# Attention loop of a hybrid decoder layer: gate products of the merge, two at a time, only ahead of the second head's transposes

## The chip, the cores and the metric

The kernel is one program on one core of a Trainium2 chip. It computes one layer of a hybrid decoder for a prompt of 1024 tokens and 8 single-token samples. The metric is the device time of one execution in microseconds (us). The engines are TensorE (PE in the profile; its weight loads are PEld), VectorE (DVE), ScalarE (ACT), GpSimd (POOL) and SyncE (SP), whose queue issues the DMAs.

## The reference, cut to what matters

Two parts of the layer meet in the stage that is changed: the sparse attention of the prompt, and the sigmoid gate of the merge, whose product with the input does not depend on the attention.

```python
h = rms_norm(x, g_pre_mix) * (1.0 + sc1) + sh1
parts = project(h, w_in, b_in)             # 'ga' and 'gb' are 1024 of its columns each
y_a, y_b, state = mix_fn(parts)            # y_b: the attention, 8 heads of 64 on 2 key groups
merged = jax.nn.sigmoid(parts['ga']) * (y_a @ w_proj_a) + jax.nn.sigmoid(parts['gb']) * (y_b @ w_proj_b)

# in the attention, for blocks of 128 queries, each head sums three softmaxes:
p_c = masked_softmax(q . kc)               # 32 compressed keys
p_s = masked_softmax(q . ks)               # all earlier blocks of keys (the sequence has 16 blocks, top 16 are taken)
p_w = masked_softmax(q . k_win)            # a window of 512 keys
out = g0 * (p_c @ vc) + g1 * (p_s @ vs) + g2 * (p_w @ v_win)
```

## The kernel before

The attention of the prompt is a list of 132 items (`items`, L290), four times 33. A group of 33 belongs to a pair of heads j = 0 to 3. Its first item is the compressed branch of both heads; then come 16 steps k = 0 to 15, each with two items, e = 0 for the first head of the pair and e = 1 for the second. Step k treats the query block i = k // 2: an even k is the window branch, an odd k the selected branch. The number of 128-key blocks (`span_of`, L295) grows with i: 1 at k = 0, 5 in most of the window steps, 8 at k = 15. All is fp32.

Each item n goes through five engines' stations, always in the order of n on every engine:

- `att_S` (L2362): the scores, on TensorE, issued two items ahead;
- `att_max` (L1699): the causal mask and the maximum, on VectorE;
- `att_exp` (L1172): the exponential with its sum, on ScalarE;
- `att_rec` (L1733) and L1015: the reciprocal of the sum on VectorE, then the scaling by it and by the branch's gate on GpSimd;
- `att_T` (L2385): 128x128 transposes of the scaled probabilities on TensorE (L2398; L2395 in the compressed branch), which wait for the scaling;
- `take_T` (L591): the transposed blocks are copied out of PSUM, groups in bank 0 by VectorE and groups in bank 1 by ScalarE (L608, L603). From step k = 8 on an item has two groups, and the first, of four blocks, is in bank 0. Below that an item has one group, and the two items of a step use the two banks in turn, the first head bank 0;
- `att_PV` (L2401): the product with the values for both heads of a step (L2415, L2420), issued once the second head's item has been transposed.

The order on VectorE is written out: for item n it takes the group of bank 0 of item n, then the reciprocal of item n + 1, then the maximum of item n + 2. On ScalarE it is the group of bank 1 of item n, then the exponential of item n + 2, then the tanh of a gate chain if one ended in item n (L1213).

TensorE has further work in this loop that does not depend on it: 18 gate chains (6 slices of 128 output columns by 3 groups of 344 tokens) of 8 products each, 144 products in all (`gate_product`, L2424). A chain accumulates in PSUM bank 7. Its first product waits until the tanh of the chain before has read that bank (`s_filla`). `gates_at`, a table made at L314 to L326, gives to each item two lists of products: those issued ahead of `att_T(n)`, and those issued ahead of `att_S(n + 2)`. The numbers of slots come from `gate_slots` (L309), and `rest` keeps a new chain from starting too soon after the last one ended. SyncE loads the weight slices of the chains into two places by turns, each when three chains have released its place.

In this text a *product* is one matmul of 344 columns; the profile records each fp32 matmul as two instructions, so that a product is "x2" there. T0 is the transposes of a first head's item, T1 those of a second head's.

Of the kernel before, what the change touches and what calls it, by code (L numbers as in the profile page):

```python
# [129 lines left out]
def build(nc, t, outs):  # L130
# [3 lines left out]
    with ExitStack() as ctx:  # L134
# [102 lines left out]
        def take(rows, *shape):  # L237
# [52 lines left out]
        items = [(j, None, None) if k is None else (j, k, e)  # L290
                 for j in range(NH // 2) for k, e in [(None, None)] + [(k, e) for k in range(2 * NT) for e in range(2)]]
        NI = len(items)
# [16 lines left out]
        def gate_slots(n):  # L309
            if items[n][1] is None:  # L310
                return (3, 3) if n == 0 else (3, 0)
            return (1, 3) if n + 2 < NI and items[n + 2][1] is None else (1, 0)

        gates_at, queue, rest = {}, [(c, c // 3, c % 3, k) for c in range(3 * MF) for k in range(KD)], 0  # L314
        for n_ in range(NI):
            gates_at[n_] = ([], [])
            for x, slots_ in enumerate(gate_slots(n_)):
                if slots_ == 1 and queue and queue[0][3] in (0, 6):
                    slots_ = 2

                while slots_ and queue and (queue[0][3] or n_ >= rest):
                    gates_at[n_][x].append(queue.pop(0))
                    slots_ -= 1
                    if gates_at[n_][x][-1][3] == KD - 1:
                        rest = n_ + 2
# [2407 lines left out]
```

How the kernel before makes its waits and increments, by code:

```python
        def freed(eng, rnd, step):  # L558
            g, k = divmod(step, KN[rnd])
            if k < KN[rnd] - 1:
                eng.wait_ge(s_rused, (0, 3 * (KN[0] - 1))[rnd] + g * (KN[rnd] - 1) + k + 1)
            else:
                eng.wait_ge(s_yps, 9 * rnd + 3 * (g + 1))
# [18 lines left out]
        def take_q(eng, copy, j, bank):  # L583
            eng.wait_ge(s_pt[bank], fills_Q[j][bank][1] + 1)
            for e in range(2):
                for half in range(2):
                    ins = copy(qT_[e][half * HD:(half + 1) * HD, bank * 512:(bank + 1) * 512], ps[e * HD:(e + 1) * HD, 4 + bank, :])
            ins.then_inc(s_ev[bank], 1)
# [1 line left out]
        def take_T(eng, copy, t, bank):  # L591
            j, k, e = items[t]
            for b, blocks, turn in fills_T[t][0]:
                if b != bank:
                    continue
                eng.wait_ge(s_pt[b], turn + 1)
                if k is None:
                    if j:
                        eng.wait_ge(s_pv, pv_before(j - 1, 2 * NT - 2) + 1)
                    else:
                        eng.wait_ge(s_kvrows, 32)
                    copy(pcT[b], ps[0:2 * NCMP, 4 + b, :]).then_inc(s_ev[b], 1)
                else:
                    u = unit_at(t)
                    if u >= 3:
                        eng.wait_ge(s_pv, (u - 3) // 2 + 1)
                    copy(ptbuf[u % 3][:, blocks[0]:blocks[-1] + 1, :],
                         ps[:, 4 + b, 0:len(blocks) * P].rearrange("p (o c) -> p o c", c=P)).then_inc(s_ev[b], 1)
```

## Time and profile before

| | |
|---|---|
| time, median of 3 runs | 2107.27 us (2101.02 to 2110.47) |
| the profiled execution | 2108.73 us, its span 2107.0 us |
| TensorE busy | 2020.4 us, 96% of the span |
| VectorE, ScalarE, GpSimd busy | 811.1, 516.6, 389.5 us |
| the chain of work that ended last | TensorE 87%, VectorE 4%, DMA 3%, ScalarE 2%, GpSimd 2% |
| the attention loop | from 466 to 846 us of the span |

The table is read with two things in mind. First, TensorE is close to saturated over the whole program, so that what counts is the idle time on it. Secondly, the share is an average over stages; the attention loop is one of those where TensorE is often released by another engine. In the views of the trace a row of the timeline is a run of like instructions on one engine: its start, its length up to the modelled end of the last, the engine, the line, what it writes and reads, the count, and in brackets the idle time ahead of it with what ended it. Since matmuls overlap, the length of a row is more than what it takes on the engine; the distance between two starts is the better measure.

### The profile page before, as it was taken

The page shows a single profiled execution, that of the slowest core. Times are in us where ns is not written, and L with a number is a line of the kernel's source. Part 1 is how long each engine was busy: PE and PEld are TensorE (multiplying, and loading weights), DVE is VectorE, ACT ScalarE, POOL GpSimd, SP SyncE. Part 2 cuts the span into 40 slices and gives each one's busy share as a digit, 9 for nine tenths or more (in the row PEclk, how much of TensorE's full clock was granted, in tenths as well). Part 3 has the DMA queues.
Part 4 walks back from the last instruction along what each step waited for, and adds up shares of the span by engine and source line. Part 5 has one row for each costly group of instructions (what it writes and reads, how often), then busy time and mean ns, then how long its engine had stood idle before and what let it go on. Part 6 is the DMA issues. An engine that isn't in the chain of part 4 may idle for free.

```text
span 2107.0 us, 28710 instructions
## 1 busy us (share of the span) xinstructions
PE 2020.4 (96%) x11391; PEld 1599.5 (76%) x11391; DVE 811.1 (38%) x1522; ACT 516.6 (25%) x938; POOL 389.5 (18%) x447
## 2 busy tenths in 40 slices
PE   6999999989999998999999998899999999999998
PEld 3588877775665565666676675899999999888876
DVE  2444333475665657521202165411111111234355
ACT  2322210134444444111200145311111111123232
POOL 0000111222232323231000046000000000155552
PEclk8999999999999999999999999999999999999999
DMA  9342001032000000564324354112112112235453
GB/s 361 114 173 101 21 23 40 1 89 80 11 11 11 8 5 11 169 169 115 97 72 130 102 178 150 61 41 60 41 40 61 40 41 61 81 122 167 150 190 111
DMA packets 172941, 184.90 MB, mean 88 GB/s; under 512 B 9893, under 2 KB 143117, under 8 KB 172366
## 3 DMA queue, kind: packets, MB, share of 16 engines
q1 hardware_dynamic: 172814, 183.12, 27.7%
q8 instruction: 91, 1.49, 0.3%
q14 instruction: 36, 0.29, 0.0%
HBM read 170.74 MB, written 16.53 MB: 89 GB/s over the span
## 4 chain that ended last, share of the span: by engine, by line
PE 87%; DVE 4%; DMA 3%; ACT 2%; POOL 2%; issue 1%; SPq 1%; POOLq 0%; ACTq 0%; DVEq 0%
PE ps L2659 23%; PE ps L2560 11%; PE ps L2163 9%; PE ps L2184 5%; PE ps L2602 5%; PE ps L2603 5%; PE ps L2604 5%; PE ps L2430 4%; PE ps L2420 3%; PE ps L2381 3%; PE ps L2398 3%; DMA arena<-in_w_ada 1%; POOL arena L1015 1%; PE ps L2123 1%; DVE arena L608 1%
## 5 line engine op out<-in xcount | busy, mean ns | idle before, releaser
L2659 PE MATMUL ps<-h_hi,wup_hi 128*128 128x344 f32 x1056 | 339.3, 321 | 9.7 <-issue 4.9
L2659 PE MATMUL ps<-h_lo,wup_hi 128*128 128x344 f32 x1056 | 339.8, 322 | 0.0
L2659 PE MATMUL ps<-h_hi,wup_lo 128*128 128x344 f32 x1056 | 339.4, 321 | 0.0
L1046 POOL CAST ra_hi<-arena 128x384 fp32r<-128x384 f32 (+1 forms) x90 | 51.6, 573 | 851.2 <-PE ps L2659 465.7
L2659 PEld LDWEIGHTS ps<-h_hi,wup_hi 128*128 128x128 f32 x1056 | 200.0, 189 | 10.6 <-issue 9.5
L2659 PEld LDWEIGHTS ps<-h_lo,wup_hi 128*128 128x128 f32 x1056 | 199.8, 189 | 0.0
L2602 PE MATMUL ps<-rw_hi,ra_hi 128*128 128x512 f32 x480 | 191.1, 398 | 8.8 <-DVE rw_lo L1885 5.7
L2659 PEld LDWEIGHTS ps<-h_hi,wup_lo 128*128 128x128 f32 x1056 | 199.5, 189 | 0.0
L2163 PE MATMUL ps<-arena,hT 128*128 128x261 f32 (+2 forms) x768 | 194.6, 407 | 3.4 <-ACT hT L1112 2.5
L2603 PE MATMUL ps<-rw_hi,ra_lo 128*128 128x512 f32 x480 | 189.1, 394 | 0.0
L2604 PE MATMUL ps<-rw_lo,ra_hi 128*128 128x512 f32 x480 | 188.3, 392 | 0.0
L2163 PEld LDWEIGHTS ps<-arena,hT 128*128 128x128 f32 x768 | 143.7, 191 | 43.2 <-issue 8.4
L1015 POOL TENSOR_SCALAR arena<-arena 128x640 f32<-128x640 f32 (+7 forms) x128 | 99.9, 781 | 280.4 <-DVE arena L1739 280.4
L1885 DVE TENSOR_TENSOR rw_lo<-hT,rw_hi 128x1024 fp32r<-128x1024 f32 x65 | 91.4, 1410 | 144.6 <-ACT rw_hi L1256 144.6
L2560 PE MATMUL ps<-hT,arena 128*128 128x344 f32 x448 | 134.5, 455 | 0.0
L1189 ACT ACTIVATE arena<-ps,arena 128x640 f32<-128x640 f32 (+7 forms) x128 | 89.6, 700 | 171.1 <-DVE arena L1719 167.7
L1052 POOL TENSOR_TENSOR ra_lo<-arena,ra_hi 128x384 fp32r<-128x384 f32 (+1 forms) x90 | 124.3, 1381 | 4.8
L2560 PEld LDWEIGHTS ps<-hT,arena 128*128 128x128 f32 x448 | 83.9, 190 | 43.6 <-issue 2.1
L2602 PEld LDWEIGHTS ps<-rw_hi,ra_hi 128*128 128x128 f32 x480 | 90.5, 189 | 33.5 <-issue 8.0
L2430 PE MATMUL ps<-hT,xn 128*128 128x344 f32 x288 | 112.0, 497 | 1.3 <-ACT arena L1213 1.2
L2560 PE MATMUL ps<-arena 128*128 128x344 f32 x352 | 112.1, 474 | 0.7 <-ACT arena L1264 0.5
L1256 ACT ACTIVATE rw_hi<-hT 128x1024 fp32r<-128x1024 f32 x65 | 68.7, 1059 | 176.8 <-DMA hT<-in_w_down 176.8
(420 smaller groups left out, 2868.6 us busy)
## 6 DMA issues: line engine op xcount, KB each, us to landing
hT<-in_w_down SPq DMA_DIRECT2D x65, 512.0 KB, 3.3
arena<-in_w_ada SPq DMA_DIRECT2D x12, 2048.0 KB, 8.2
arena<-in_w_up SPq DMA_DIRECT2D x44, 512.0 KB, 4.6
arena<-in_w_out SPq DMA_DIRECT2D x24, 512.0 KB, 3.9
arena<-in_w_in SPq DMA_DIRECT2D x19, 512.0 KB, 4.4
arena<-in_cache_cmp_kv SPq DMA_DIRECT2D x64, 128.0 KB, 2.1
arena<-in_cache_slc_kv SPq DMA_DIRECT2D x128, 64.0 KB, 1.9
arena<-in_w_in SPq DMA_DIRECT2D x4, 1544.0 KB, 13.5
```

The source lines that it names most:

```text
L1015: nc.gpsimd.tensor_scalar(pbuf[u % 3][:, 0:nb * P], pbuf[u % 3][:, 0:nb * P], rec[:, u % 4:u % 4 + 1], gts[:, i, col:col + 1], ALU.mult, A ...
L1052: nc.gpsimd.tensor_tensor(lo[:, 0:n], src[:, k, cols], hi[:, 0:n], ALU.subtract).then_inc(s_ra, 1)
L1189: nc.scalar.activation(pbuf[u % 3][:, 0:n], sp_[:, 512 - n // 2:512 + n // 2], ACT.Exp, bias=nmx[:, u % 4:u % 4 + 1], accum_out=rsum[:, u ...
L1885: nc.vector.tensor_tensor(rw_lo[rnd][at][:, :], rw_from(rnd, step), rw_hi[rnd][at][:, :], ALU.subtract).then_inc(s_rlo, 1)
L2163: ins = nc.tensor.matmul(ps[:, bank, 0:width], hT[:, k, n * P:(n + 1) * P], w[:, k, 0:width], start=(k == 0), stop=(k == KD - 1))
L2184: ins = nc.tensor.matmul(ps[:, mix_bank(j, n), 0:PA], h[:, k, :], w[:, k, :], start=(k == 0 and x == 0), stop=(k == KD - 1 and x == 2))
L2430: ins = nc.tensor.matmul(ps[:, 7, 0:TG], wfill[m % 2][:, k, :], hT[:, k, q * TG:(q + 1) * TG], start=(k == 0), stop=(k == KD - 1))
L2560: ins = nc.tensor.matmul(ps[:, bank, 0:TG], w[:, k, :], src[:, k, q * TG:(q + 1) * TG], start=(k == 0), stop=(k == kn - 1))
L2602: nc.tensor.matmul(out, ra_hi[rnd][a][:, rows], rw_hi[rnd][w][:, cols], start=first, stop=False)
L2603: nc.tensor.matmul(out, ra_lo[rnd][a][:, rows], rw_hi[rnd][w][:, cols], start=False, stop=False)
L2604: ins = nc.tensor.matmul(out, ra_hi[rnd][a][:, rows], rw_lo[rnd][w][:, cols], start=False, stop=last)
L2659: ins = nc.tensor.matmul(ps[:, bank, 0:TG], w[:, k0 + k, :], h[:, k, toks], start=(k == 0 and j == 0), stop=(k == KD - 1 and j == 2))
```

## The change

`gate_slots` gave one slot to every item, and now gives two slots to items with e = 1 and none to items with e = 0. The rule that stretched a slot at the beginning and the end of a chain stretched 1 to 2 at products 0 and 6, and now stretches 2 to 3 at products 0 and 5, so that a chain is issued as 3 + 2 + 3. `rest` keeps its value, but a chain may now start one item sooner after it. The three slots of a compressed item and the three ahead of the scores that cross into the next pair stay.

```diff
         def gate_slots(n):
             if items[n][1] is None:
                 return (3, 3) if n == 0 else (3, 0)
-            return (1, 3) if n + 2 < NI and items[n + 2][1] is None else (1, 0)
+
+            two = 2 * items[n][2]
+            return (two, 3) if n + 2 < NI and items[n + 2][1] is None else (two, 0)
...
-                if slots_ == 1 and queue and queue[0][3] in (0, 6):
-                    slots_ = 2
-
-                while slots_ and queue and (queue[0][3] or n_ >= rest):
+                if slots_ == 2 and queue and queue[0][3] in (0, 5):
+                    slots_ = 3
+
+                while slots_ and queue and (queue[0][3] or n_ >= rest - 1):
```

From this table the 144 products fall out as follows. Before, they stand in 100 runs of one to three, 128 products in the first three pairs and 16 in the fourth, up to its step k = 6. Now they stand in 54 runs of two or three, and all of them are in the first three pairs. The run ahead of the transposes of the second and third pair's compressed item is 2 and 0 products long before, and 3 and 3 now.

TensorE in the second pair, steps k = 11 and 12, from a T0 to the PV behind the next T0. L2398 is the transposes, L2381 the scores, L2415 and L2420 PV, L2430 products. Before:

```order
L2398 MATMUL ps<-const,arena 128x128 x6
L2381 MATMUL ps<-arena 128x320 x2
L2415 MATMUL ps<-arena 64x128 x2
L2420 MATMUL ps<-arena 64x128 x10
L2430 MATMUL ps<-hT,xn 128x344 x2
L2398 MATMUL ps<-const,arena 128x128 x6
L2381 MATMUL ps<-arena 128x320 x2
L2430 MATMUL ps<-hT,xn 128x344
L2398 MATMUL ps<-const,arena 128x128 x5
L2381 MATMUL ps<-arena 128x448 x2
L2420 MATMUL ps<-arena 64x128 x12
```

And now (all lines are two further on):

```order
L2400 MATMUL ps<-const,arena 128x128 x6
L2383 MATMUL ps<-arena 128x320 x2
L2417 MATMUL ps<-arena 64x128 x2
L2422 MATMUL ps<-arena 64x128 x10
L2432 MATMUL ps<-hT,xn 128x344 x2
L2400 MATMUL ps<-const,arena 128x128 x6
L2383 MATMUL ps<-arena 128x320 x2
L2400 MATMUL ps<-const,arena 128x128 x5
L2383 MATMUL ps<-arena 128x448 x2
L2422 MATMUL ps<-arena 64x128 x12
```

The product between the scores behind T1 and the next T0 is gone. (The order has each product once, the trace twice.)

TensorE where the second pair ends and the third begins: the last T0, the transposes of the queries (L2359), products, the compressed scores (L2372), PV, the last T1, and the compressed branch's transposes (L2395). Before:

```order
L2398 MATMUL ps<-const,arena 128x128 x8
L2359 MATMUL ps<-const,arena 128x128 x8
L2430 MATMUL ps<-hT,xn 128x344 x3
L2372 MATMUL ps<-arena 128x32 x16
L2415 MATMUL ps<-arena 64x128 x2
L2420 MATMUL ps<-arena 64x128 x10
L2430 MATMUL ps<-hT,xn 128x344 x2
L2398 MATMUL ps<-const,arena 128x128 x8
L2381 MATMUL ps<-arena 128x64 x2
L2395 MATMUL ps<-const,arena 64x128 x8
```

And now:

```order
L2400 MATMUL ps<-const,arena 128x128 x8
L2361 MATMUL ps<-const,arena 128x128 x8
L2432 MATMUL ps<-hT,xn 128x344 x3
L2374 MATMUL ps<-arena 128x32 x16
L2417 MATMUL ps<-arena 64x128 x2
L2422 MATMUL ps<-arena 64x128 x10
L2432 MATMUL ps<-hT,xn 128x344 x3
L2400 MATMUL ps<-const,arena 128x128 x8
L2383 MATMUL ps<-arena 128x64 x2
L2432 MATMUL ps<-hT,xn 128x344 x3
L2397 MATMUL ps<-const,arena 64x128 x8
```

Three products now stand ahead of the compressed branch's transposes; and the three behind PV begin a new chain, where the two before ended one.

## Rows read from the trace of the kernel before

**Rows 1.** The page's first part: busy time, share of the span, instructions.

```profile
PE 2020.4 (96%) x11391; PEld 1599.5 (76%) x11391; DVE 811.1 (38%) x1522; ACT 516.6 (25%) x938; POOL 389.5 (18%) x447
```

**Rows 2.** Busy time by stretch: engines, granted clock, DMA share, GB/s.

```profile
760.00:780.00 20.00, 17.93 (x128) 11.78 (x128) 11.01 (x37) 7.37 (x25) 3.95 (x8) 0.91 0.01 1
...
800.00:846.00 46.00, 37.06 (x341) 24.24 (x343) 33.16 (x75) 19.46 (x50) 15.07 (x16) 1.00 0.00 1
466.00:846.00 380.00, 352.66 (x2639) 224.09 (x2640) 235.25 (x567) 157.05 (x421) 99.92 (x128) 0.98 0.08 23
```

**Rows 3.** Who waited for whom, 465 to 846 us: total, times, longest.

```profile
PE ps L2398 <- POOL arena L1015: 14.6, 26, 1.0
```

**Rows 4.** The chain that ended last, fourth pair, step k = 9.

```profile
809.05 0.60 PE ps L2398 x4
...
809.68 0.69 DVE arena L608
...
810.54 0.88 POOL arena L1015
```

**Rows 5.** Timeline of TensorE, second pair, k = 11 and 12: start, length, count, idle.

```profile
626.01 0.85 PE L2430 MATMUL ps<-hT,xn 128*128 128x344 f32 x2
626.69 0.82 PE L2398 MATMUL ps<-const,arena 128*128 128x128 f32 x6
...
628.18 0.85 PE L2430 MATMUL ps<-hT,xn 128*128 128x344 f32 x2
629.12 0.76 PE L2398 MATMUL ps<-const,arena 128*128 128x128 f32 x5
...
634.50 0.84 PE L2430 MATMUL ps<-hT,xn 128*128 128x344 f32 x2
635.55 0.98 PE L2398 MATMUL ps<-const,arena 128*128 128x128 f32 x7 [0.20 <-POOL arena L1015]
```

**Rows 6.** The same, two T0 without a product ahead (k = 11, k = 14).

```profile
527.62 0.87 PE L2398 MATMUL ps<-const,arena 128*128 128x128 f32 x6 [0.98 <-POOL arena L1015]
...
642.50 0.76 PE L2398 MATMUL ps<-const,arena 128*128 128x128 f32 x5 [0.76 <-POOL arena L1015]
```

**Rows 7.** The same, at k = 6 and 7: T1 behind two products, then T0.

```profile
597.02 1.42 PE L2430 MATMUL ps<-hT,xn 128*128 128x344 f32 x4
598.28 0.60 PE L2398 MATMUL ps<-const,arena 128*128 128x128 f32 x4
598.81 0.70 PE L2381 MATMUL ps<-arena 64*128 64x256 f32 x4
599.44 0.66 PE L2398 MATMUL ps<-const,arena 128*128 128x128 f32 x4
```

**Rows 8.** Timeline where the third pair begins.

```profile
659.08 1.42 PE L2430 MATMUL ps<-hT,xn 128*128 128x344 f32 x4
659.77 0.60 ACT L1180 ACTIVATE arena<-ps 128x512 f32<-128x512 f32 x1 [4.35 <-DVE ps L1709]
660.34 1.04 PE L2398 MATMUL ps<-const,arena 128*128 128x128 f32 x8
...
663.80 1.92 PE L2395 MATMUL ps<-const,arena 128*64 128x128 f32 x8 [2.06 <-DVE arena L1731]
```

**Rows 9.** The tanh of the gate chains, 600 to 700 us: shortest, median, longest in ns.

```profile
L1213 ACT ACTIVATE arena<-ps,arena x6: 537/538/539, 601.3 to 695.8; 128x344 f32<-128x344 f32 x6
```

**Rows 10.** Timeline at the second pair's k = 1: scores, then the scaling of that item.

```profile
572.25 0.44 PE L2381 MATMUL ps<-arena 64*128 64x64 f32 x4
...
574.15 0.45 POOL L1015 TENSOR_SCALAR arena<-arena 128x128 f32<-128x128 f32 x1 [0.88 <-DVE arena L1739]
```

**Rows 11.** Timeline of TensorE, the fourth pair's head: first T0, then k = 6 and 7.

```profile
768.63 0.27 PE L2398 MATMUL ps<-const,arena 128*128 128x128 f32 x1
...
792.08 0.70 PE L2381 MATMUL ps<-arena 64*128 64x256 f32 x4
...
795.80 0.66 PE L2398 MATMUL ps<-const,arena 128*128 128x128 f32 x4 [0.65 <-POOL arena L1015]
```

## The prediction, made before the changed kernel ran

> **What bounds the kernel now.** I read the page first: TensorE is busy for 96% of the span [rows 1], so any work is dear there, and any idle time. Then the busy times by stretch: in the attention loop, 466 to 846 us, TensorE is busy for 352.66 of 380 us [rows 2]; the idle 27 us are what the order of the gate products can lose or win. The waits say what ends this idle time: above all GpSimd's scaling, ahead of the transposes [rows 3]. The chain that ended last shows how that comes about in the fourth pair, where no products are left. The first four blocks of T1 are followed by VectorE's copy (0.69 us), the reciprocal, GpSimd's scaling (0.88 us) and then T0 [rows 4]. VectorE must copy T1's group before it may take the reciprocal that T0 needs. From T1's start to the end of the scaling this takes 810.54 + 0.88 - 809.05 = 2.37 us, and all that TensorE has to put in between are the rest of T1 and the scores of one item. From T0 to T1 it is the other way round: there PV stands in between, over a us long, and T1 finds its data ready. So from step k = 9 on T0 is the place that waits, and T1 isn't. The change takes the products away from the place that waits and gives them to the one that doesn't.
>
> **What a product costs.** A single product ahead of T1, where nothing is waited for, takes 626.69 - 626.01 = 0.68 us [rows 5]. Two in a row take 598.28 - 597.02 = 1.26 us [rows 7]. So a further product of a run costs 0.58 us, and a run costs 0.10 us on top, for the interruption.
>
> **What the wait of T0 costs.** Without a product ahead the idle time is 0.98 us, and 0.76 us at k = 14, where fewer blocks are scaled [rows 6]. A T that doesn't wait starts before the modelled end of the scores, 599.44 against 598.81 + 0.70 [rows 7]; these 0.07 us add to the wait: 1.05 and 0.83 us. For k = 12, a window step as well, I take the value between, 0.94. With one product ahead T0 starts 0.94 to 1.05 us after the product's start, where 0.68 would do [rows 5], so 0.26 to 0.37 us remain. Two products leave nothing. In other words the wait hides the first product entirely: at T0 a product is free, at T1 it is paid in full.
>
> **The change, part by part**, against the profiled execution of 2108.7 us.
>
> 1. The fourth pair gives its 16 products to the first three. Each lengthens a run there: 16 x 0.58 = **+9.3 us**.
>
> 2. The first three pairs have 88 runs before and 54 now: 34 x 0.10 = **-3.4 us**.
>
> 3. T0 at k = 9 to 15 in three pairs is 21 places. Before, 12 have one product (nine wait 0.37, three 0.26 us), 6 have two or more (nothing), and 3 have none (1.05 + 0.83 + 1.05): 3.3 + 0.8 + 2.9 = 7.0 us. Now none has one: 5 x 1.05 + 0.94 + 0.83 = 7.0 us for a pair, 21.0 for three. **+14.0 us**. This is the term that decides. That products ahead of T1 don't help T0 is seen at the k = 11 place of rows 6: T1 before it had two products ahead, as now everywhere, and T0 waited 0.98 us. The path to T0 starts at T1's first transposes, behind those products.
>
> 4. Up to k = 8 I take nothing for T0. There T1's only group is in bank 1 and goes to ScalarE, so VectorE isn't held. In rows 7 T0 follows T1 and the scores with no product ahead, with no idle time, since two products stood ahead of T1. All such places look like this one now.
>
> 5. The compressed branch's transposes wait for a row of VectorE's small operations, 663.80 - 660.34 = 3.46 us after the T before. For 2.06 of them TensorE is idle where no product stands between [rows 8]. Three products (0.10 + 3 x 0.58 = 1.8 us) fit in. The second pair's have two before and three now, the third pair's none and three, so that 4 more are hidden: 4 x 0.58 + 0.1 = **-2.4 us**.
>
> 6. A new wait arises ahead of these. The chain that ends ahead of the compressed scores is now followed by the next one right behind PV, and that must wait for its tanh, which stands behind the compressed exponential on ScalarE. That ended at 659.77 + 0.60 = 660.37 [rows 8], and the tanh takes 0.54 us [rows 9], so the product could start at 661.0 instead of 659.08: 1.9 us. Behind it in TensorE's order stand T1 and all else. At the second pair's start the same order arises; bounds are nothing, if PV there runs at the lower clock and covers the path, and 1.9. I take 1.3: **+3.2 us** for both. The other chains start as long after the last tanh as before. Of the 26 waits of rows 3 one or two lie outside T0, near the start, and get covered: **-0.5 us**.
>
> 7. What the fourth pair gains by losing its 16 products. Three of them, at its boundary, took full price: 0.68 + 1.26 = 1.9 us. The other 13 lie between 768.63 and 795.80, 27.2 us [rows 11]. Without them an item is bound by its own path from scores to transposes. That is 574.15 + 0.45 + 0.04 - 572.25 = 2.4 us for one block of keys [rows 10] and 795.80 - 792.08 = 3.7 us for four [rows 11]; between them I take 2.8 and 3.3. The next scores of the same head stand behind its T (0.2 to 0.5 us). The seven periods are then 2.6 + 3.0 + 3.1 + 3.6 + 3.7 + 4.1 + 4.2 = 24.3 us, which saves 2.9 and not the 8.5 that 13 products and their 10 runs cost. Bounds: 0 and 8.5. Sum: **-4.9 us** (2.9 + 1.9, rounded up for a low clock there).
>
> No DMA is added. The weight slices are asked for a little sooner, with the chains; each is used three chains later. VectorE, ScalarE and GpSimd do the same work in the same order, but for the place of the tanh; nothing waits for that but the next chain.
>
> The sum: 9.3 - 3.4 + 14.0 - 2.4 + 3.2 - 0.5 - 4.9 = **+15.3 us**, 2124.0 us for the profiled execution. The median of the runs is 2107.3 us, 1.4 below it, so 2122.6.
>
> **The rivals.**
>
> *The head of the fourth pair gives back the full price.* If TensorE's work and not the path through the other engines bounds it, term 7 is -10.4 us and the sum +9.8: 2117 us. For it: some periods there held two and three products and still waited for nothing. Against it: the fourth pair at k = 7, where the products have just run out, waits 0.65 us [rows 11].
>
> *The clock falls in the fourth pair's head.* With products in it the stretch from 760 to 780 us was granted 0.91 of full speed, so the lower of the two levels (1.2 of 2.4 GHz) was there for a part of it [rows 2]. Transposes and scores would take twice their time in each period, 0.3 us at one block of keys and 0.9 at four, some 4.3 us over the seven periods: +19.6, so 2127 us. Against it speaks that from 800 to 846 us, without any product, TensorE was busy for 37.06 of 46 us and granted 1.00 [rows 2]. The Trainium skill ("TensorE: Matmul & The Clock Gate", Part 4) says that transposes don't count as busy for the clock in the way that matmuls do. By that rule the clock would fall wherever products are gone and transposes remain; the row at 800 us doesn't bear it out, in a mix with scores and PV.
>
> *Faster: T0 doesn't wait any more.* If T0 were bound by its own scores' path, two products between those scores and T0 would cover it as one on either side did, as up to k = 8. Then term 3 is -7.0 instead of +14.0, and the sum -5.7: 2101.6 us. The point from which it decides: the path T1, copy, reciprocal, scaling must be no longer than T1 and the scores behind it, some 1.4 us (0.7 for each), and the chain shows 2.37 [rows 4]. Rows 6 speak against it twice, since products stood ahead of both T1.
>
> **How the numbers follow.** The forecast has a chance of 0.62, with 2116 to 2129 us as its own range (terms 6 and 7 by their bounds, and some 3 us by which runs of the same kernel differ). The full price given back has 0.17; the falling clock 0.12; faster 0.04; 0.05 is left for what I don't see. The likeliest is the forecast, 2122.5 us. The range has to reach the first rival (2117) and the second (2127) with the differences of runs: 2113 to 2130. What a measurement of this kernel can tell from no change is about 0.5%, 10.5 us, so the bound of slower is 2117.8. The forecast is nearly all above it; the first rival lies at it and goes mostly to "same". Slower 0.78, same 0.18, faster 0.04.
>
> **What the profile after would show.** The transposes' wait for the scaling [rows 3] should grow by more than 10 us, with nearly all T0 from k = 9 on showing about 0.98 us idle, and T1 none. The third pair's compressed transposes should lose their 2.06 us idle, and the product run ahead of the T before them should gain about 1.9 us, released by ScalarE. From the first T0 of the fourth pair to that of k = 7 it should take 24 to 25 us instead of 27.2. I am wrong if T0 at k = 9 to 15 starts without idle time, or if the idle time moves there but the first three pairs don't get longer by some 20 us.

## The result and the profile after

The changed kernel takes 2134.33 us (median of 4 runs, 2131.68 to 2136.59), the kernel before 2108.87 us in the same comparison: the ratio is 1.0121, with a 95% interval of 1.0102 to 1.0140. It is slower by 25 us, where 15 had been forecast. The direction and the largest term, the waits of T0 from k = 9 on, were right; the time lies above the range (2113 to 2130).

The page's first part after, as [rows 1] before, and the busy times by stretch, as [rows 2] (length, then busy time of TensorE, its weight loads, VectorE, ScalarE, GpSimd, the granted clock, DMA share, GB/s). The loop now runs from 466 to 872 us:

```profile
PE 2030.1 (95%) x11391; PEld 1608.3 (75%) x11391; DVE 807.6 (38%) x1522; ACT 517.5 (24%) x938; POOL 389.6 (18%) x447
```

```profile
466.00:872.00 406.00, 359.68 (x2648) 231.28 (x2648) 234.88 (x568) 157.70 (x421) 100.40 (x128) 0.95 0.07 21
786.00:806.00 20.00, 17.07 (x106) 11.26 (x106) 10.26 (x35) 6.39 (x23) 4.04 (x8) 0.59 0.00 0
806.00:826.00 20.00, 18.08 (x126) 10.53 (x122) 11.57 (x32) 8.75 (x25) 6.10 (x9) 0.80 0.01 2
826.00:872.00 46.00, 37.22 (x344) 24.38 (x346) 33.08 (x76) 19.50 (x50) 14.96 (x16) 1.00 0.00 1
```

The loop is 26 us longer. TensorE is idle in it for 406 - 359.7 = 46 us, where it was 27 us in [rows 2], and busy for 7 us more, with the same instructions: a larger part of them ran at the lower clock. The granted clock over the loop is 0.95 instead of 0.98, that is, the lower level for 41 us of it instead of 17. It is lowest in the fourth pair's first half, which no longer has products.

The wait of the transposes for the scaling, as [rows 3] (14.6 us, 26 times, before):

```profile
PE ps L2400 <- POOL arena L1017: 33.3, 41, 1.0
```

The timeline of TensorE in the second pair, k = 11 and 12, the place of [rows 5] (start, length, engine, line, count, and the idle time ahead in brackets):

```profile
638.13 0.87 PE L2400 MATMUL ps<-const,arena 128*128 128x128 f32 x6 [0.98 <-POOL arena L1017]
...
641.28 1.42 PE L2432 MATMUL ps<-hT,xn 128*128 128x344 f32 x4
642.54 0.82 PE L2400 MATMUL ps<-const,arena 128*128 128x128 f32 x6
643.28 0.81 PE L2383 MATMUL ps<-arena 64*128 64x320 f32 x4
644.97 0.33 PE L2400 MATMUL ps<-const,arena 128*128 128x128 f32 x1 [0.87 <-POOL arena L1017]
```

TensorE is idle for 0.98 and 0.87 us ahead of the two T0, as in [rows 6], though two products stand ahead of the T1 between them. And where the third pair begins, the place of [rows 8]:

```profile
678.46 2.00 PE L2432 MATMUL ps<-hT,xn 128*128 128x344 f32 x6 [1.71 <-ACT arena L1215]
680.30 1.04 PE L2400 MATMUL ps<-const,arena 128*128 128x128 f32 x8
...
681.63 2.00 PE L2432 MATMUL ps<-hT,xn 128*128 128x344 f32 x6
683.76 1.06 PE L2397 MATMUL ps<-const,arena 128*64 128x128 f32 x8
```

The compressed transposes still start 683.76 - 680.30 = 3.46 us after the T before. The three products fill what was idle; the run ahead waits 1.7 us for the tanh.

### The profile page after: what moved, and what is told of

The parts are those of the page before. It is cut to its first block, busy times and chain, and to the rows that moved or that the text cites. A ratio compares the mean times of both kernels' runs of the same rounds, so it can differ in the third digit from the quotient of the medians.

```text
span 2134.5 us, 28710 instructions
## 1 busy us (share of the span) xinstructions
PE 2030.1 (95%) x11391; PEld 1608.3 (75%) x11391; DVE 807.6 (38%) x1522; ACT 517.5 (24%) x938; POOL 389.6 (18%) x447
## 3 DMA queue, kind: packets, MB, share of 16 engines
q1 hardware_dynamic: 172814, 183.12, 27.5%
## 4 chain that ended last, share of the span: by engine, by line
PE 84%; DVE 5%; DMA 3%; POOL 2%; ACT 2%; issue 2%; SPq 1%; POOLq 0%; DVEq 0%; ACTq 0%
PE ps L2661 22%; PE ps L2562 11%; PE ps L2165 9%; PE ps L2186 5%; PE ps L2604 5%; PE ps L2605 5%; PE ps L2606 5%; PE ps L2432 3%; PE ps L2422 3%; PE ps L2400 3%; PE ps L2383 2%; POOL arena L1017 2%; DMA arena<-in_w_ada 1%; PE ps L2125 1%; DVE arena L610 1%
## 5 line engine op out<-in xcount | busy, mean ns | idle before, releaser
L2400 PE MATMUL ps<-const,arena 128*128 128x128 f32 x528 | 86.4, 289 | 34.1 <-POOL arena L1017 33.3
L2400 PEld LDWEIGHTS ps<-const,arena 128*128 128x128 f32 x528 | 60.9, 144 | 76.6 <-POOL arena L1017 61.8
## 6 DMA issues: line engine op xcount, KB each, us to landing
arena<-in_w_in SPq DMA_DIRECT2D x4, 1544.0 KB, 13.4
```

The lines of the kernel that those rows point to most:

```text
L2400: ins = nc.tensor.transpose(ps[:, 4 + b, x * P:(x + 1) * P], pbuf[unit_at(t) % 3][:, o * P:(o + 1) * P], ident)
```

## The experiments

Each has its edit against the changed kernel or the kernel before, as said. Times of all are medians; the kernel before took 2110.5 us beside the first four, 2109.8 beside the next four and 2108.0 beside the last. What a run took more or less than the changed kernel is therefore a difference of two comparisons, between which the kernel before itself moved by 1 to 2 us; a difference of that size says nothing.

### The mirror: products ahead of T0, none ahead of T1

```diff
-            two = 2 * items[n][2]
+            two = 2 * (1 - items[n][2])
```

> The mirror of the change: two products (three at a chain's ends) ahead of the first head's transposes (T0), none ahead of the second head's (T1). My theory is that T0 at k = 9 to 15 waits 1.05 us for the path T1, copy, reciprocal, scaling wherever no product stands ahead of it, and T1 does not wait. Then the 21 waits of the first three pairs (21 us in the changed kernel) vanish behind the products, T1 stays without idle time from k = 9 on, and the kernel takes about 20 us less than the changed one, 2114 us, some 5 us above the kernel before, since the fourth pair still has no products. The rival, that it is the grouping into runs of two and three, or the emptied fourth pair, that costs the time, and not the side on which they stand, expects 2130 us or more.

It took 2121.24 us (ratio to before 1.0051, 1.0024 to 1.0077), 13 us less than the changed kernel. No T0 of the first three pairs waits any more; the wait of all transposes for the scaling is halved:

```profile
PE ps L2400 <- POOL arena L1017: 16.4, 26, 1.1
```

So the side counts, and the rival that it is only grouping or the empty fourth pair falls. The gain is 7 us short of what I expected. By the trace some 6 us of waits of T1 have come up in the first three pairs, all at k = 0 to 6. The lower clock is granted for 53 us of the loop instead of 41, and the fourth pair's stretch from its first T0 to that of k = 7 takes 30.3 us, 23.9 of them at the lower clock, where the changed kernel takes 28.3 with 17.3.

### One product back to T0

```diff
         assert not queue, len(queue)
+        for n_ in range(1, 3 * PAIR):
+            k_, e_ = items[n_][1:]
+            if k_ is None or k_ < 9 or e_:
+                continue
+            if gates_at[n_ - 1][0] and gates_at[n_ - 1][0][-1][3] != KD - 1:
+                gates_at[n_][0].append(gates_at[n_ - 1][0].pop())
```

> The changed kernel, but in the first three pairs, from k = 9 on, 15 of the 21 first head's transposes (T0) get the last product of the run ahead of the second head's (T1). By my theory T0 starts at the same time after T1 with or without this product (the wait of 1.05 us hides its 0.68 us), while each run ahead of T1 is 0.58 us shorter: 15 x 0.58 = 8.7 us less than the changed kernel, 2125.6 us. If T0's wait were no path of its own but followed the products, as a rival has it, nothing would be gained: 2134 us.

It took 2125.41 us, 8.9 us less than the changed kernel, for 15 products moved by one place. The timeline of TensorE in the second pair has both sorts of T0 (here L2407, products L2439), the first with a product ahead, the second without:

```profile
620.35 0.81 PE L2390 MATMUL ps<-arena 64*128 64x320 f32 x4
621.09 0.85 PE L2439 MATMUL ps<-hT,xn 128*128 128x344 f32 x2
622.14 0.76 PE L2407 MATMUL ps<-const,arena 128*128 128x128 f32 x5 [0.21 <-POOL arena L1024]
...
627.66 0.81 PE L2390 MATMUL ps<-arena 64*128 64x320 f32 x4
629.45 0.76 PE L2407 MATMUL ps<-const,arena 128*128 128x128 f32 x5 [0.98 <-POOL arena L1024]
```

From the start of the scores ahead (620.35 and 627.66) it is 1.79 us to T0 in both cases. The product at T0 costs nothing, and what it cost at T1 is gained.

### The last 16 products in the fourth pair again

```diff
-                while slots_ and queue and (queue[0][3] or n_ >= rest - 1):
+                if queue and queue[0][0] == 16 and n_ < 3 * PAIR + 1:
+                    continue
+                if n_ > 3 * PAIR:
+                    slots_ = 0 if x else 1 + (queue[:1] != [] and queue[0][3] in (0, 6))
+
+                while slots_ and queue and (queue[0][3] or n_ >= rest - (n_ <= 3 * PAIR)):
```

> The changed kernel, but its last two chains (16 products) are issued in the fourth pair, where the kernel before had them, and the third pair's end has none. In the changed kernel the fourth pair gained nothing from losing them: from its first T0 to that of k = 7 it took 28.2 us, against 27.2 before, at a granted clock of 0.59 and 0.80 in the 40 us around it. If the products there are free (the path through the other engines bounds it, and the clock falls without them), this takes 16 x 0.58 + 6 x 0.1 = 9.9 us off the third pair and gives nothing back: 2124 us, and the clock in the fourth pair's first half is back to 0.9 or more. If products cost there what they cost elsewhere, it takes the same time as the changed kernel, 2134 us.

It took 2128.49 us, 5.8 us less. From the fourth pair's first T0 to that of k = 7 it takes 27.2 us with 13 more products in it, against 28.3 without them, so they are free there. The clock from 780 to 826 us, which was 0.67 in the changed kernel:

```profile
780.00:826.00 46.00, 42.65 (x302) 27.41 (x300) 26.09 (x75) 18.48 (x55) 11.54 (x18) 0.90 0.05 13
```

Of the 9.9 us that I expected, 7.7 are in the third pair; 1.4 go again between its last T0 and the fourth pair's first. Two products stand ahead of that T0 now (1.26 us), while the three taken from the crossing had been hidden: the compressed scores there wait 2.58 us for the queries, where they waited 0.85. The lower clock is no part of it, with 13.7 us here and 13.4 in the changed kernel. The first two pairs, where this program is the changed kernel's own, took 4.3 us more in this profile than in that one (216.7 against 212.4, from the first compressed transposes to those of the third pair); the lower clock was granted for 18 us of them instead of 7. That is how much two executions of one program can differ here.

### Sixteen idle matmuls in the fourth pair

Nobody reads their result; the kernel is else the changed one.

```diff
+            spare = dict(zip(range(3 * PAIR + 1, 3 * PAIR + 14), (2, 1, 1, 1, 1, 2, 0, 2, 1, 1, 1, 1, 2)))
...
                 for x in gates_at[n][0]:
                     gate_product(*x)
+                for y in range(spare.get(n, 0)):
+                    if n == 3 * PAIR + 1 and y == 0:
+                        pe.wait_ge(s_filla, 3 * MF)
+                    nc.tensor.matmul(ps[:, 7, 0:TG], ident, hT[:, y, 0:TG], start=True, stop=True)
```

> The changed kernel with 16 further matmuls of 344 columns, whose result nobody reads, in the fourth pair at the places where the kernel before had its last 16 products. If the fourth pair's first half is bound by the path through the other engines and by a clock that falls when TensorE has too little to do, these cost nothing or less than nothing: 2132 to 2135 us, granted clock 0.9 or more there, 27.2 us from its first T0 to that of k = 7. If they cost their full price it is 10 us more, 2144 us.

It took 2132.48 us for 16 matmuls more. The 1.9 us below the changed kernel are within what its own runs differ by (2131.68 to 2136.59), but 10 us more, their full price, are excluded. The two stretches that had 0.59 and 0.80 now read:

```profile
786.00:806.00 20.00, 18.92 (x130) 12.36 (x132) 9.97 (x35) 6.75 (x25) 4.31 (x9) 0.91 0.00 0
806.00:826.00 20.00, 18.24 (x139) 11.14 (x137) 12.57 (x33) 8.69 (x24) 6.36 (x9) 1.00 0.01 2
```

From the first T0 to that of k = 7 it takes 27.1 us, about as in [rows 11] (27.2), and the changed kernel 28.3. In this stretch the work is more and the time is less: without matmuls in between, TensorE's clock falls here, and its transposes and scores, which lie on the path from item to item, take longer. The products that the change took away from here had kept the clock up.

### The reciprocal ahead of the copy

VectorE takes the reciprocal of item n + 1 first and copies the transposed group of item n then. Once in the changed kernel, once in the kernel before:

```diff
-                take_T(dve, nc.vector.tensor_copy, n, 0)
                 if n + 1 < NI:
                     att_rec(n + 1)
+                take_T(dve, nc.vector.tensor_copy, n, 0)
```

> The changed kernel, but VectorE takes the reciprocal of item n + 1 before it copies the transposed group of item n out of PSUM. If T0's wait of 1.05 us is the path T1's first group, copy (0.69 us), reciprocal, scaling, it shrinks by the copy to some 0.36 us at its 28 places (k = 9 to 15 of all four pairs): 28 x 0.69 = 19 us less, 2115 us. The rival, that T0 waits for the way of its own scores through mask, maximum and exponential, expects no gain: 2134 us.

> The kernel before with the same exchange on VectorE. Its waits for this path are 7.0 us in the first three pairs and 7.0 us in the fourth. A place with one product ahead has 0.26 to 0.37 us left, which vanish; one without a product has 1.05, of which 0.69 vanish: 4.0 + 3 x 0.69 + 7 x 0.69 = 10.9 us less, 2099 us. The rival expects 2110 us.

In the changed kernel it took 2138.25 us (3.9 more), in the kernel before 2111.31 us (ratio 1.0013, 1.0000 to 1.0026). Neither gained. Yet the wait of T0 from k = 9 on fell as the path says, in the first three pairs: from 7.0 to 3.2 us a pair in the changed kernel, from 2.0 to 1.0 in the kernel before. Below k = 9 it grew, from 1.2 to 2.4 us a pair in the changed kernel and from nothing to 0.5 in the kernel before. In the fourth pair it grew from k = 9 on as well, from 7.0 to 9.9 us in both. The timeline of the fourth pair at k = 9, exchanged order in the changed kernel:

```profile
828.62 0.79 ACT L1191 ACTIVATE arena<-ps,arena 128x640 f32<-128x640 f32 x1 [1.75 <-DVE arena L1721]
...
829.53 0.16 DVE L1741 RECIPROCAL arena<-arena 128x1 f32<-128x1 f32 x1 [0.95 <-ACT arena L1191]
...
829.79 0.87 POOL L1017 TENSOR_SCALAR arena<-arena 128x640 f32<-128x640 f32 x1 [1.91 <-DVE arena L1741]
...
830.72 0.76 PE L2400 MATMUL ps<-const,arena 128*128 128x128 f32 x5 [1.28 <-POOL arena L1017]
```

Here the reciprocal waits for the exponential of its own item; VectorE stands still for 0.95 us, and all behind it comes later. So both theories hold, each in its place. With products ahead of T1 the copy was the last to hold T0 up. Without any, T0's own scores are just as late, and the exchange only moves the copy behind a wait. The queries' transposes at the crossing into the third pair now wait 1.7 us for that copy, where it was 0.35 in the changed kernel:

```profile
666.37 1.97 PE L2361 MATMUL ps<-const,arena 128*128 128x128 f32 x8 [1.73 <-DVE arena L610]
```

### No chain starts right behind the crossing

```diff
-                while slots_ and queue and (queue[0][3] or n_ >= rest - 1):
+                while slots_ and queue and (queue[0][3] or n_ >= rest - 1 + (n_ % PAIR == PAIR - 1 and queue[0][3] == 0)):
```

> The changed kernel, but no gate chain starts between the crossing into a pair and its compressed item, so that the last T1 of the first and second pair no longer stands behind a wait for the tanh (0.6 and 1.8 us in the changed kernel's trace). Everything behind it comes three products later and fills the third pair's crossing. I expect the two waits gone and 2132 us, 2 to 3 us less than the changed kernel; no less if the wait was hidden by another one there.

It took 2141.41 us as a median, 9 us above what I expected, but its six runs lie from 2129.7 to 2143.5 and the profile is of the fastest. The two shorter runs (2129.7 and 2132.2) were granted 0.981 and 0.979 of the clock over the span, the four longer ones 0.974 to 0.975. In it the wait has only gone elsewhere, to the third pair's crossing, where a chain now starts right ahead of the compressed transposes:

```profile
679.41 3.08 PE L2432 MATMUL ps<-hT,xn 128*128 128x344 f32 x6 [3.53 <-ACT arena L1215]
```

What this wait costs by itself is not told apart by this run. That the four other runs are about 12 us longer goes with their lower clock; why the clock differs from run to run, it does not show.

### A table by what the runs had shown

Against the kernel before: from k = 9 on two products ahead of T0 and none ahead of T1, one ahead of each item below that.

```diff
-            return (1, 3) if n + 2 < NI and items[n + 2][1] is None else (1, 0)
+            own = 1 if items[n][1] < 9 else 2 * (1 - items[n][2])
+            return (own, 3) if n + 2 < NI and items[n + 2][1] is None else (own, 0)
...
-                if slots_ == 1 and queue and queue[0][3] in (0, 6):
+                if slots_ == 1 and queue and queue[0][3] in (0, 6) and items[n_][1] < 9:
```

> A table by what the runs have shown so far: from k = 9 on two products ahead of T0 and none ahead of T1; below that one ahead of each item, as in the kernel before; three ahead of the compressed transposes; and 27 products left for the fourth pair. 21 of 28 long T0 then have products ahead. Against the kernel before, the waits of T0 from k = 9 on fall from 14 to some 6 us, those of the compressed transposes by 2 to 4 us, and there are 10 runs fewer (1 us): 2110.5 - 11 = 2099 us, with the clock of the fourth pair's first half at 0.9 or more. If only the sum of products counts, and not where they stand, 2110 us.

It took 2098.85 us (ratio 0.9956, 0.9940 to 0.9972), as expected. Of the 28 long T0, 22 have products ahead. The wait for the scaling in its loop, and the clock in the stretch from 760 to 806 us:

```profile
PE ps L2399 <- POOL arena L1016: 7.1, 9, 1.0
```

```profile
760.00:806.00 46.00, 44.75 (x325) 27.68 (x321) 28.89 (x75) 20.67 (x59) 14.58 (x20) 1.00 0.04 12
```

Then the same, with the products stretched to the loop's end:

```diff
-                return (3, 3) if n == 0 else (3, 0)
-            return (1, 3) if n + 2 < NI and items[n + 2][1] is None else (1, 0)
+                return (5, 3) if n == 0 else (3, 0)
+            own = 1 if items[n][1] < 9 else 2 * (1 - items[n][2])
+            return (own, 4) if n + 2 < NI and items[n + 2][1] is None else (own, 0)
...
-                if slots_ == 1 and queue and queue[0][3] in (0, 6):
+                if slots_ == 1 and queue and queue[0][3] == 6 and x == 0 and items[n_][1] is not None and n_ // PAIR < 3:
```

> The spread table carried on to the end of the fourth pair: two products ahead of 27 of the 28 long T0 (one ahead of the others at least), at most one ahead of each item below k = 9 and two at a chain's end, three ahead of the compressed transposes, five ahead of the first, four at one crossing. Against the spread table (2098.9 us) the five T0 of the fourth pair that still waited 1 us each are covered (4.9 us), two products are hidden at the first compressed item (1.2 us), and there are 8 runs more (0.8 us): 2094 us. The last chain ends only at the last item but one, so the merge's first weights are asked for some 50 us later; if they land late, 1 to 4 us come back. A rival: the products moved out of the earlier steps let the clock fall there, and nothing is gained.

It took 2088.56 us, where the kernel before took 2108.04: ratio 0.9907, 0.9890 to 0.9924. It is the fastest version, 46 us below the changed kernel, with the same 144 products. Its table gives two products to 24 of the 28 long T0 and one to the other four. The waits for the scaling are nearly gone, and the loop is over before 830 us:

```profile
PE ps L2399 <- POOL arena L1016: 1.9, 5, 0.6
```

Against the kernel before it gains 19.5 us, and the table before it 11.0; of these 8.5 us more I had expected 5. The lower clock is granted for 13 us of its loop, against 24 there; the rival that the clock would fall in the thinned steps was wrong. The merge's first product starts 0.37 us after TensorE is free, as before, so its weights aren't late.

## Why the prediction was right or wrong

The profiled spans differ by 2134.5 - 2107.0 = 27.5 us. Step by step, with the forecast of the prediction's terms:

**The wait of T0 from k = 9 on (term 3, +14.0)** was right to the row: all 21 places show 0.98, 0.87 (k = 12) and 0.76 us (k = 14) idle, with the 0.07 of the overlap 7.0 us a pair. The mirror and the product put back show that it is the missing product that counts, and the exchange on VectorE that the copy is on its path. The rival that T0 would not wait is refuted.

**T0 below k = 9 (term 4, nothing)** was wrong. In each of the first three pairs T0 at k = 3 waits 0.66 us (0.59 idle and the 0.07 of the overlap), at k = 1 0.2 to 0.6 and at k = 6 0.17: 3.5 us in all, against 0.1 before. The timeline at the second pair's k = 2 and 3 shows why (all engines, changed kernel):

```profile
588.11 0.49 PE L2383 MATMUL ps<-arena 64*128 64x128 f32 x4
...
588.90 0.49 PE L2383 MATMUL ps<-arena 64*128 64x128 f32 x4
...
590.04 0.16 DVE L1741 RECIPROCAL arena<-arena 128x1 f32<-128x1 f32 x1 [0.30 <-ACT arena L1191]
590.12 0.28 DVE L1715 TENSOR_TENSOR ps<-ps,const 128x128 f32<-128x128 f32 x1
...
592.37 0.44 PE L2400 MATMUL ps<-const,arena 128*128 128x128 f32 x2 [0.59 <-POOL arena L1017]
```

With no product between them, the scores of two items follow each other within 0.8 us. The second item's mask (590.12) must then queue on VectorE behind the first one's reciprocal, which waits for the first one's exponential. I had looked at the item's own path, and at places in the kernel before where two products stood ahead of T1; but there a product stood elsewhere and had kept the scores apart. The first table by what the runs had shown, with one product ahead of each item below k = 9 again, bears this out: no T0 below k = 9 waits in its trace.

**The fourth pair (term 7, -4.9)** was the largest miss. From the last T0 of the third pair to the last T1 of the loop it took 96.9 us, against 96.1 before: +0.8, so 5.7 us of the gap. The stretch of [rows 11] took 28.3 us instead of the 24.3 I had summed from the path, which is 4.0 of them. Another 1.6 lie at the crossing, from the third pair's last T0 to the fourth's first: 20.7 us against 21.0 before, where 1.9 less had been forecast. The lower clock was granted for 13.4 us of it instead of 6.8.

The clock rival named the cause, with 0.12 of the chance. Its price, 4.3 us, is about what is missing in the stretch, and the idle matmuls show it, for they bring both the clock and the 27.1 us back. The mirror allows a second look: its fourth pair has no products either and the same order of instructions, but the lower clock fell on other steps of it. The same step at both levels, from T0 at k = 6 to T0 at k = 7, first in the changed kernel, then in the mirror:

```profile
817.31 0.66 PE L2400 MATMUL ps<-const,arena 128*128 128x128 f32 x4 [0.73 <-POOL arena L1017]
...
821.62 0.66 PE L2400 MATMUL ps<-const,arena 128*128 128x128 f32 x4 [0.64 <-POOL arena L1017]
```

```profile
801.29 1.11 PE L2400 MATMUL ps<-const,arena 128*128 128x128 f32 x4
...
806.63 0.66 PE L2400 MATMUL ps<-const,arena 128*128 128x128 f32 x4
```

And the stretches in them, the mirror's first:

```profile
801.00:806.00 5.00, 5.00 (x26) 3.08 (x25) 3.00 (x7) 1.56 (x4) 1.03 (x2) 0.51 0.00 0
817.00:822.00 5.00, 3.76 (x31) 2.45 (x32) 3.41 (x8) 2.21 (x6) 1.80 (x3) 1.00 0.00 0
```

At the full clock the step takes 4.31 us and TensorE waits in it; with the lower clock for 4.6 us of it, it takes 5.34, and TensorE is never idle. There TensorE itself is the path. I had summed 4.2 for this step. At k = 0 and 1 the mirror was at the full clock and took 2.67 and 3.06 us, where I had 2.6 and 3.0. In the changed kernel 3.6 of the missing 4.0 us stand in the steps k = 2 to 5, 18.1 us long, and the lower clock was granted for 14.9 of these. So the steps of the prediction that failed are term 7 and, with 3.4 us, term 4. Term 7 summed the fourth pair at the full clock, while 17.3 of the stretch's 28.3 us ran at the lower one; the sum of the path was nearly right where it can be seen. At k = 2 to 4 no run shows the path at the full clock without products.

I had weighed the row from 800 to 846 us, where the clock stays full without products, too heavily: it is the end of the pair, with 5 to 8 blocks a step, and the changed kernel shows the same there (1.00 from 826 us on). The place in question is its beginning, with 1 to 4 blocks. By the rule of the Trainium skill ("TensorE: Matmul & The Clock Gate", Part 4) transposes don't count as busy for the clock as matmuls do. The traces don't show this to be the cause: from 786 to 806 us, at 0.59, the transposes are 18 of TensorE's 106 instructions, and from 826 to 872 us, at 1.00, they are 92 of 344, a larger part.

**The compressed transposes and the tanh (terms 5 and 6, -2.4 and +3.2)**: the idle 2.06 us shrank to 0.13, and the tanh wait was 0.5 and 1.7 us idle at the two crossings, 2.2 where 3.2 had been forecast. Chain starts below k = 9 waited 0.5 us in each of three places, about what they had waited before (1.2 us in all). From the first compressed transposes to the last T0 of the third pair all terms but the fourth pair's came to +20.2 us, and the traces show +24.5; with 3.4 for term 4, 0.9 us is left, and its cause stays open. The lower level was granted for 6.8 us between these points in either profile, though in other places.

**Outside of the loop** the first transposes came 0.6 us later and the stages behind it took 1.6 us more. The program is the same there. From the last T1 of the loop to the end the profiles of this study take 1259.6 to 1266.3 us, before 1263.4 and after 1265.0, so that this is no effect of the change that can be told from chance.

15.3 + 3.4 + 0.9 + 5.7 + 0.6 + 1.6 = 27.5 us. The rival of the full price given back is refuted too: taking the products away from the fourth pair's beginning gave nothing back, and cost 1.1 us there.

The range failed because it had the falling clock as a rival by itself and nothing at all for T0 below k = 9. The forecast with both, 2122.5 + 4.3 + 3.4 = 2130.2 us, stands already at its upper end. The two are separate: with the idle matmuls the fourth pair's clock is back, and T0 at k = 3 of the first three pairs still waits.

## What to carry to other kernels

Filler work for a saturated engine belongs ahead of the instruction that waits, and there a wait of 1.05 us hides all of one product (0.68 us), or most of two (1.26 us); which of two alternating places waits is read from the chain, by what the other engines do in order between them. Here the filler also kept the scores of successive items apart and, in the fourth pair's first half, the clock up, so it had to last until there: spread over all four pairs and put ahead of the waiting transposes, the same 144 products gave 19.5 us instead of costing 25. How much of that is due to the side, to the spreading and to the clock, no run tells apart. A row that shows the clock at full without filler speaks for its own mix of sizes only.

## What the runs showed of the hardware

Sixteen fp32 matmuls of 344 columns added to a stretch of small transposes and scores made it shorter: 27.1 instead of 28.3 us, at a granted clock of 0.91 and 1.00 instead of 0.59 and 0.80 in its two parts. The same instructions in the same order, without filler, took 4.31 us at the full clock and 5.34 with the lower one for 4.6 us of it. And the lower clock comes at places that differ between executions of one program: the same two pairs took 212.4 us in one profile and 216.7 in another.
